# Loading the weights of a streaming encoder layer: two 512 KB slabs per transfer instead of one, from the fifth slab on

## The reference

```
n = rmsnorm(h); u = n @ w_in          # q, k, v of two attention mixers, forget logits, two gates
m = sigmoid(gate_A) * (o_A @ w_a_proj) + sigmoid(gate_B) * (o_B @ w_b_proj);  h += m @ w_o
h += relu(rmsnorm(h) @ w_up)^2 @ w_down
h += (p @ w_ple_proj) * sigmoid(rmsnorm(h) @ w_ple_gate)
y = rmsnorm(h)
```

## Time and profile before

| | us |
|---|---|
| median of 3 runs | 1885.02 |
| lowest, highest | 1884.65, 1885.55 |
| the profiled execution, its own time | 1885.35 |
| its span, first to last instruction | 1883.3 |

### The profile page before, as it was taken

One profiled execution on the slowest core, in us unless ns is written; L12 is line 12 of the kernel. 1 busy time (PEld: TensorE's weight loads), 2 busy tenths in 40 slices (PEclk: granted clock), 3 DMA queues, 4 the chain that ended last, 5 costly groups with the idle time before them and its releaser, 6 DMA issues.

```text
span 1883.3 us, 35145 instructions
## 1 busy us (share of the span) xinstructions
PE 1875.3 (100%) x12809; PEld 1871.4 (99%) x12809; DVE 986.3 (52%) x1504; ACT 709.9 (38%) x883; POOL 180.9 (10%) x282
## 2 busy tenths in 40 slices
PE   9999999999999999999999999999999999999998
PEld 9999999999999999999999999999999999999998
DVE  8766666674444445555444344434444444455554
ACT  6333333343333333333332333323333233333554
POOL 0111111110000001221100001000100001122122
PEclk9999999999999999999999999999999999999999
DMA  7544444445444444444444444444444444444442
GB/s 264 174 168 166 163 166 165 165 149 201 156 134 156 156 149 141 150 148 155 152 156 142 150 144 148 156 155 135 156 146 157 142 149 144 153 152 141 155 156 100
DMA packets 94294, 292.42 MB, mean 155 GB/s; under 512 B 13056, under 2 KB 26520, under 8 KB 94104
## 3 DMA queue, kind: packets, MB, share of 16 engines
q1 hardware_dynamic: 75744, 275.32, 44.6%
q10 hardware_dynamic: 18520, 16.69, 2.9%
HBM read 284.08 MB, written 9.46 MB: 156 GB/s over the span
## 4 chain that ended last, share of the span: by engine, by line
PE 99%; DMA 0%; DVE 0%; ACT 0%; issue 0%; SPq 0%; DVEq 0%; ACTq 0%
PE banks L404 32%; PE banks L405 32%; PE banks L406 32%; PE banks L472 0%; PE banks L474 0%; PE banks L473 0%; PE banks L424 0%; PE banks L425 0%; DMA h<-in_x_t 0%; PE banks L576 0%; PE banks L575 0%; PE banks L577 0%; PE banks L448 0%; PE banks L447 0%; PE banks L450 0%; PE banks L449 0%
## 5 line engine op out<-in xcount | busy, mean ns | idle before, releaser
L651 ACT ACTIVATE w_hi<-w_raw 128x1024 fp32r<-128x1024 f32 x510 | 539.2, 1060 | 985.8 <-PE banks L406 978.3
L404 PE MATMUL banks<-x_hi,w_hi 128*128 128x320 f32 x2512 | 780.2, 311 | 0.0
L406 PE MATMUL banks<-x_hi,w_lo 128*128 128x320 f32 x2512 | 776.2, 309 | 0.0
L405 PE MATMUL banks<-x_lo,w_hi 128*128 128x320 f32 x2512 | 776.1, 309 | 0.0
L965 DVE TENSOR_TENSOR w_lo<-w_raw,w_hi 128x1024 fp32r<-128x1024 f32 x510 | 602.5, 1217 | 20.7 <-ACT w_hi L651 20.2
L405 PEld LDWEIGHTS banks<-x_lo,w_hi 128*128 128x128 f32 x2512 | 471.6, 188 | 0.2
L404 PEld LDWEIGHTS banks<-x_hi,w_hi 128*128 128x128 f32 x2512 | 471.6, 188 | 0.2
L406 PEld LDWEIGHTS banks<-x_hi,w_lo 128*128 128x128 f32 x2512 | 471.5, 188 | 0.0
L404 PE MATMUL banks<-o_hi,w_hi 128*128 128x320 f32 x1280 | 395.6, 309 | 0.0
L405 PE MATMUL banks<-o_lo,w_hi 128*128 128x320 f32 x1280 | 395.5, 309 | 0.0
L406 PE MATMUL banks<-o_hi,w_lo 128*128 128x320 f32 x1280 | 395.5, 309 | 0.0
(11 more groups left out here) (162 smaller groups left out, 1088.1 us busy)
## 6 DMA issues: line engine op xcount, KB each, us to landing
w_raw<-in_w_slabs SPq DMA_DIRECT2D x515, 512.0 KB, 4.0
out_kv_t<-k_t ACTq DMA_DIRECT2D x16, 160.0 KB, 2.7
out_kv_t<-v_t ACTq DMA_DIRECT2D x16, 160.0 KB, 2.9
h<-in_x_t ACTq DMA_DIRECT2D x1, 2560.0 KB, 10.4
out_y<-y_rows SPq DMA_DIRECT2D x4, 512.0 KB, 3.4
h<-in_x_t SPq DMA_DIRECT2D x3, 640.0 KB, 9.6
f_keys<-f_rows ACTq DMA_DIRECT2D x8, 224.0 KB, 4.0
bias_rows<-in_rel_rows ACTq DMA_DIRECT2D x1, 1024.0 KB
```

Of the source, the lines that this page charges most:

```text
L404: nc.tensor.matmul(out, w_hi[:, slot, ws], hi[:, xs], start=k == lo_k, stop=False)
L405: nc.tensor.matmul(out, w_hi[:, slot, ws], lo[:, xs], start=False, stop=False)
L406: mm = nc.tensor.matmul(out, w_lo[:, slot, ws], hi[:, xs], start=False, stop=k == hi_k)
L651: nc.scalar.activation(w_hi[:, slot, :], w_raw[:, slot, :], ACT.Copy).then_inc(s_whi, 1)
```

## The change

From slab 4 on, SP issues one load for both slabs of a panel: 1 MB from two neighbouring slabs of the weight tensor into two neighbouring places of `w_raw`, each partition receiving 4 KB of the one and 4 KB of the other. It waits once for it, until VectorE has made `w_lo` of both slabs that were in these places. The load counts on the semaphore of the first of the two places alone. ScalarE therefore waits for that semaphore for either slab, so for the whole 1 MB before it copies the first. The loop still has 128 turns, now with two loads in each. The first four slabs are loaded as before. No other engine's program is changed.

```diff
-            for s in range(SLOTS, first):
-
-                sp.wait_ge(s_wlo, s - SLOTS + 1)
-                load_slab(w[s], s % SLOTS)
+
+            def load_pair(pair, slot):
+
+                sp.dma_start(w_raw[:, slot:slot + 2, :], pair.rearrange("s p n -> p s n")).then_inc(s_slab[slot], 16)
+
+            for s in range(SLOTS, first, 2):
+
+                sp.wait_ge(s_wlo, s - SLOTS + 2)
+                load_pair(w[s:s + 2], s % SLOTS)
             with sp.Fori(0, (slabs - first) // SLOTS) as i:
-                for j in range(SLOTS):
+                for j in range(0, SLOTS, 2):
                     s = first + j
-                    split = sp.snap(i * SLOTS + (s - SLOTS + 1))
+                    split = sp.snap(i * SLOTS + (s - SLOTS + 2))
 
                     sp.wait_ge(s_wlo, split)
-                    load_slab(w[bass.ds(i * SLOTS + s, 1)].rearrange("a p n -> (a p) n"), s % SLOTS)
+                    load_pair(w[bass.ds(i * SLOTS + s, 2)], s % SLOTS)
...
-                    act.wait_ge(s_slab[slot], t.loads())
+                    act.wait_ge(s_slab[slot - half], t.loads())
...
-                act.wait_ge(s_slab[s % SLOTS], 16 * (s // SLOTS + 1))
+                act.wait_ge(s_slab[s % SLOTS if s < SLOTS else s % SLOTS // 2 * 2], 16 * (s // SLOTS + 1))
```

## The result

| | before | changed |
|---|---|---|
| median us | 1884.99 | 1888.69 |
| lowest, highest | 1884.65, 1885.55 | 1886.72, 1890.44 |
| runs | 20 | 20 |
| profiled execution, own time | 1885.35 | 1887.07 |
| its span | 1883.3 | 1885.0 |

The changed kernel takes 3.70 us more, a ratio of 1.0018 with a 95% interval of 1.0012 to 1.0024. That is 0.196%, by 0.1 us under the 3.8 us (0.2%) that the prediction took for the least that can be told from no change, but it is clear of the scatter: the quickest run of the changed kernel (1886.72) is slower than the slowest of the old one (1885.55). The median lies outside the range of 1883.8 to 1887.0. Two more things have to be explained: the changed kernel's runs lie 3.7 us apart where the old ones lie 0.9 apart, and the one trace is of a run of 1887.07, only 1.72 above the trace of before.

The account below looks back on a forecast made before the run. The prediction took TensorE's matmuls to bound the kernel, with no load holding them up. Its terms summed to 0 + 0 + 0 + 0 against the profiled 1885.35, giving a forecast median of 1885.0 us, range 1883.8 to 1887.0.

Parts of the forecast that it names:

- What bounds the kernel: Whole kernel: PE is the bound, matmuls fill 1875.3 of 1883.3 us, and no load has held it up from slab 4 on.
- the fourth row: One of PE's four single waits in the profile before the change, which the prediction put at 2.6 us together.
- L, the landing of 1 MB: Time for a paired slab load to land: taken as 4.9 us, with 3.0 and 9.0 kept as bounds.
- twice as long: SP's issue of 1 MB: if double, 0.33 us more per panel before the landing, carried in the bounds.
- Room in the channel mixer: 128 panels, output projection alike: pair lands 2.6 us ahead of ACT; cost 0, at L = 9.0 too.
- at the second load of x: Pair issued at 438.3 lands at 447.2; PE has 4.7 us in hand; cost 0.
- at the start: Slabs 4 and 5 land at 19.0, 1.5 us ahead of ACT; cost 0 for L up to 8.0.
- Room in a unit: Sixteen attention units, tightest place: ACT waits 1.9 us, PE stalls only from L = 7.6; cost 0 at 4.9.
- The first rival: Attention units: with L over 7.6, PE stalls in each of 14 units, 20 us at L = 9.0, so 1905; chance 0.05.
- The sum: Whole kernel: 0 + 0 + 0 + 0 against the profiled 1885.35; forecast 1885.0, the median being 0.33 lower.
- its reason for "same": Whole kernel: the no-stall forecast, chance 0.91, in which the later loads cost PE nothing.
- What would show it: Profile signs: 256 loads of 1024 KB landing in 4.5 to 5.5 us, PE's waits still four, 2.6 us, span 1883.

Follow-up runs that it names:

- the two waits alone: Two runs against the kernel before: 512 KB loads issued only when both places are free, 1885.50 us; ScalarE waiting for both slabs, loads issued early, 1885.49 us.
- the filled one: The changed kernel with 16 unread identity transposes put on PE ahead of its waits for the last attention: 1887.24 us.

## Why the prediction was wrong

**What bounds the kernel**: right, and read too loosely. PE is the bound and no load held it up. But the fourth row, 0.2 us before L446, was the mark of a place where PE had caught up with the chain that feeds it. I counted it as one of four small waits and never asked what chain it was. Room there was not small but nothing.

**L, the landing of 1 MB**: 4.9 taken, 4.9 measured (median; 4.7 at the place that decides). The fit of the Trainium skill, "DMA: Bandwidth & Descriptors", section on the anatomy of one DMA, makes an estimate of 4.4, for another issuing path; the measurement decides. An issue takes 0.37 us where one of 512 KB took 0.33, so "twice as long" wasn't so.

**Room in the channel mixer, at the second load of x, at the start**: right. In the channel mixer ScalarE's splits still wait for PE. At the second load of x ScalarE waited 5.3 us and DVE 0.2, and PE for nothing. The pair of slabs 4 and 5 landed at 18.8, where 19.0 was forecast.

**Room in a unit**: this step failed. It says "sixteen, 23.5 us each", takes one unit from the loop and concludes "So nothing behind it moves until L = 111.69 - 1.06 - 105.2 = 5.4". That rests on both slabs being split in one go, so that the second slab's wait for PE hides the first one's lateness. It holds for the fourteen turns in which the program has that order (`unit`). For the turn behind them, at the head of the merge, the code (in the lines ahead of `merge(Panel(T_MERGE + 3), 1)`) has another: one half, then the attention output. There the room ends at L = 390.7 - 387.9 = 2.8 us, below the quickest 512 KB load (3.0), and L was 4.7: ScalarE was 2.0 us late, and PE waited 2.0 us more. The last sentence there, "Behind the unit's other pairs stands nothing on ACT that PE wants within a panel of time", is wrong in the same place.

**The first rival** had the right chain (a late split, the attention output, probabilities, PE) and the wrong place and count: once, not 14 times, and from L of 2.8 instead of 7.6. Its "only there is the room under 3 us" was wrong by the prediction's own numbers too: at the start it is 8.0 - 5.2 = 2.8. The rule named beside it (the Trainium skill, "Perfetto Trace Analysis", section DMA Optimizations: with the DMA engines mostly idle, splitting may let some start sooner) is borne out here: with 512 KB loads the reader starts 2.0 us sooner, and it is the one reader for which that matters. It is the separate issue and the separate wait that give this, as two 512 KB loads issued and waited for together start it at 392.83, no sooner than the pair.

**The sum** lacked a second term, the clock. A standstill of PE was priced at its length. It was 2.0 us more in the first trace, and in most runs about 1.55 behind it: 3.6, with 3.6 and 3.7 measured. With the 2.0 alone the median would have been 1887.0, at the end of the range. That the median missed the prediction's own line of 3.8 us for "slower" by 0.1 is luck: its reason for "same" was that nothing stalls.

**What would show it**: the loads came as forecast (256 of 1024 KB, which land in 4.9 us, and three of 512), but PE's four waits are 4.6 us together, not 2.6, and the span is 1885.0. ScalarE's idle time put down to DMA was forecast at 25 to 50 us and is 120.3 in 34 waits. That is a way of counting: the whole of an idle time goes to what ended it, so a wait that ran 2.4 us for PE and another 1.9 for the load counts 4.33 for the load, as in the row at 109.85, and the forecast had one such wait in a unit where most have two. The total before this line hardly changed, 986.5 us against 985.8.

## What to carry to other kernels

When a load or any input is made later, find the shortest path from it to the bounding engine in every stretch with a program of its own: the first and the last turn of a loop written out by hand are where the order differs. A wait of the bounding engine, however short, can mark a chain with no room, and a small lateness there passes through whole: here 2.0 us of ScalarE became 2.0 of PE. If a chain must be late, giving TensorE something to do meanwhile can save the clock; better is to move the waiting instruction behind what is urgent, which here made the pairs free.

## What the runs showed of the hardware that I had not expected

- TensorE's granted clock fell to its lower level after a single standstill of 1.7 to 2.3 us in a kernel that had kept it busy for 400 us, stayed there for 3.4 us, which cost 1.55, and rose again. It fell in some executions and not in others of the same kernel: in the traces after standstills of 2.29 and 1.74 us, not after 2.15 and 2.04. What decides it, these runs don't settle. Standstills of 0.6 to 0.8 us (the two waits alone, and the filled one) show only one group of runs.
- The one trace of a kernel may show the rarer kind of execution: the first had none of the clock's loss, and its own time (1887.07 beside a median of 1888.69) was the hint.
- With the pairs the weight queue has 71648 packets instead of 75744, which is 16 fewer for each of the 256 transfers saved, and its share of the 16 DMA engines' time fell from 44.6% to 42.1%. The fall isn't shown to come from size or packets: the two runs that issue two 512 KB loads one behind the other have all 75744 packets and shares of 39.9% and 39.8%, and the early issue with the wait for both has 44.5%. So a later issue alone lowers the share, by more than the pairs do; the reason isn't shown. A lower share gains no time here.
